# Seven products of half size for pairs 4 to 10 in the first part of the third gated feed-forward stage

## What is computed

```python
f = rmsnorm(h, norm_ffn_g[i])
h = h + (jax.nn.silu(f @ w_gate[i]) * (f @ w_up[i])) @ w_down[i]
```

## Time and profile before

| | us |
|---|---|
| median of 3 runs | 2271.45 |
| lowest, highest | 2271.45, 2273.67 |
| profiled execution | 2273.23 |
| its span | 2272.0 |

### The profile page before, as it was taken

The page is one execution under the profiler, slowest core; times in us unless marked ns, Lnnn a source line. Parts: engine busy times, 40 slices in busy tenths (PEclk is TensorE's granted clock), DMA queues, the critical chain, the costliest instruction groups (busy, mean ns, idle before and its releaser), DMA issues.

```text
span 2272.0 us, 38521 instructions
## 1 busy us (share of the span) xinstructions
PE 2245.7 (99%) x15555; PEld 2017.7 (89%) x15555; DVE 1399.7 (62%) x2549; ACT 1028.0 (45%) x1890; POOL 98.3 (4%) x171
## 2 busy tenths in 40 slices
PE   9999999999999999999999999999999999999998
PEld 7798999999997898999899788978899888888997
DVE  5356576759743465667588566869454465455663
ACT  5256554447533465543376443223244444223652
POOL 3001100000000001000000000100000000000001
PEclk9999999999999999999999999999999999999999
DMA  6545776245434436632365272743222222223651
GB/s 212 157 129 150 187 186 180 98 143 173 135 95 124 116 113 161 196 106 96 115 173 161 81 203 76 189 111 102 93 66 65 66 93 93 93 96 119 185 167 51
DMA packets 90132, 292.78 MB, mean 129 GB/s; under 512 B 12721, under 2 KB 16723, under 8 KB 89187
## 3 DMA queue, kind: packets, MB, share of 16 engines
q1 hardware_dynamic: 79587, 215.69, 29.6%
q0 software_dynamic: 9792, 73.57, 14.0%
q10 hardware_dynamic: 576, 1.05, 0.1%
HBM read 288.14 MB, written 71.34 MB: 158 GB/s over the span
## 4 chain that ended last, share of the span: by engine, by line
PE 88%; DVE 7%; ACT 3%; issue 2%; DMA 0%; POOL 0%; SPq 0%; DVEq 0%; ACTq 0%; POOLq 0%
PE G L1349 61%; PE G L1386 8%; PE G L1459 7%; DVE wL L2334 2%; PE X L1386 1%; PE X L1671 1%; PE X L1626 1%; PE X L1753 1%; PE X L1649 1%; ACT wH L1799 1%; DVE Av L2696 1%; DVE Av L2699 1%; PE X L1737 1%; PE X L1454 1%; PE X L1722 1%
## 5 line engine op out<-in xcount | busy, mean ns | idle before, releaser
L1799 ACT ACTIVATE wH<-raw 128x512 fp32r<-128x512 f32 (+3 forms) x648 | 459.0, 726 | 503.1 <-PE G L1349 429.9
L2334 DVE TENSOR_TENSOR wL<-raw,wH 128x512 fp32r<-128x512 f32 (+3 forms) x648 | 521.3, 815 | 224.8 <-ACT wH L1799 222.0
L1349 PE MATMUL G<-aH,wH 128*128 128x264 f32 (+2 forms) x2112 | 548.2, 321 | 4.4 <-DVE wL L2334 4.1
L1349 PE MATMUL G<-aL,wH 128*128 128x264 f32 (+2 forms) x2112 | 526.5, 311 | 0.0
L1349 PE MATMUL G<-aH,wL 128*128 128x264 f32 (+2 forms) x2112 | 526.2, 311 | 0.0
L1349 PEld LDWEIGHTS G<-aH,wH 128*128 128x128 f32 x2112 | 346.1, 189 | 35.6 <-issue 10.1
L1349 PEld LDWEIGHTS G<-aH,wL 128*128 128x128 f32 x2112 | 344.0, 188 | 22.0
L1349 PEld LDWEIGHTS G<-aL,wH 128*128 128x128 f32 x2112 | 344.6, 188 | 19.1 <-issue 0.2
L2493 DVE TENSOR_TENSOR hT<-G,hT 128x528 f32<-128x528 f32 (+1 forms) x83 | 58.0, 699 | 166.8 <-PE G L1349 166.7
L1386 PE MATMUL G<-seven,wH 128*128 128x264 f32 (+2 forms) x792 | 146.7, 284 | 1.3 <-DVE wL L2334 1.2
L1349 PE MATMUL G<-hidH,wH 128*128 128x264 f32 (+1 forms) x528 | 140.8, 321 | 3.3 <-DVE wL L2334 2.6
(11 more groups left out here) (401 smaller groups left out, 3788.3 us busy)
## 6 DMA issues: line engine op xcount, KB each, us to landing
raw<-weights SPq DMA_DIRECT2D x210, 512.0 KB, 3.7
weight_sums<-weights POOLq DMA_DIRECT2D x72, 704.0 KB, 6.7
raw<-weights SPq DMA_DIRECT2D x48, 704.0 KB, 4.1
raw<-weight_sums SPq DMA_DIRECT2D x132, 256.0 KB, 3.0
raw<-weights SPq DMA_DIRECT2D x99, 256.0 KB, 2.9
weight_sums<-weight_sums POOLq DMA_DIRECT2D x24, 704.0 KB, 4.8
raw<-weights SPq DMA_DIRECT2D x12, 384.0 KB, 6.0
negc<-sums POOLq DMA_DIRECT2D x16, 264.0 KB, 5.7
```

Of the source, the lines that this page charges most:

```text
L1349: done = e.matmul(m.pair(i)[0:M, bank, 0:n], a[:, k, 0:M], b[:, kx, lo - t0:lo - t0 + n], start=(k == 0 and c == 0), stop=(k == nk - 1 and ...
L1799: e.activation(m.high(i)[:, c], m.raw(i)[:, c], ACT.Copy).then_inc(s.w_hi, 1)
L2334: e.tensor_tensor(m.low(i)[:, c], m.raw(i)[:, c], m.high(i)[:, c].bitcast(F32), ALU.subtract).then_inc(s.w_lo, 1)
```

## The change

`SEVEN[2]` goes from 11 to 4: in the first half of the third stage pairs 4 to 10 are made by seven products each. The plain tiles of pairs 0 to 3 stay. The operands are now made in the first half: `early_operands` puts `norm7`, `sum7` and the halves of operands 1, 2, 5 and 6 beside plain tiles `u2` 1 to `g2` 3, and `last_operands` puts the low half of 6 and both halves of 7, 3 and 4 beside the first products, since those lie over `aH` and `aL`, which the plain tiles read. The sources that lay in `low` lie in `scratch`, a part of `hid2H` and `hid2L` that pairs 7 to 10 fill later. The `d2` tiles of the first half have no operand steps beside them any more. The weight sums of seven pairs are added: 32 transfers of 448 KB, and `EVERY` is changed for the last 64.

```diff
-SEVEN = {0: 11, 1: 11, 2: 11}
+SEVEN = {0: 11, 1: 11, 2: 4}
-EVERY = (1.4, 2.5, 3.2)
+EVERY = (1.4, 2.5, 2.3, 2.3)
...
-        for jj in range(0 if half else 11):
+        for jj in range(0 if half else SEVEN[f]):
...
-        for jj, p in by_seven(11 * half):
+        for jj, p in by_seven(0 if half else SEVEN[f]):
...
     def seven():
+        last = deque()
+        if ROLE[state["next"]][1:3] == (2, 0):
+            last.extend(last_operands(2))
...
             for what in splits_at(i):
                 step(*what)
+            if last:
+                for what in last.popleft():
+                    step(*what)
...
+    def early_operands():
+        n, c = [("norm7", 2, j) for j in range(8)], [("sum7", 2, p) for p in (5, 6, 7, 3)]
+        h, w = [("high7", 2, p) for p in (1, 2, 5, 6)], [("low7", 2, p) for p in (1, 2, 5)]
+        return [{2: n[0], 4: n[1], 6: n[2]}, {2: n[3], 4: n[4], 6: n[5]}, {1: n[6], 3: n[7], 6: c[0]}, {2: c[1], 5: c[2]},
+                {1: c[3], 2: h[0], 5: w[0], 6: h[1]}, {1: w[1], 2: h[2], 5: w[2], 6: h[3]}]
+
+    def last_operands(f):
+        return [[(kind + "7", f, p) for kind, p in group] for group in (
+            (("low", 6), ("high", 7)), (("high", 3),), (("low", 7),), (("high", 4),), (("low", 3),), (("low", 4),))]
...
             for half in range(2):
-                if half:
-                    yield from seven()
-                else:
+                if not half:
                     yield from fm(hold=True)
                     yield from fm(hook=("rms", ("ffn2",)))
-                    for _ in range(20):
-                        yield from fm()
-                made = [] if half else operands(2)
+                    for made in early_operands():
+                        yield from fm(before=made)
+                yield from seven()
                 for j in range(8 - half):
-                    yield from fm(before=made[j] if j < len(made) else {})
+                    yield from fm()
...
     def high7(f, p):
         e.wait_ge(s.seven_in, SUMS_IN["norm7", f, 7] if p in (1, 2, 4) else SUMS_IN["sum7", f, p])
+        if f == 2 and p in LYING:
+            e.wait_ge(s.chunk, AT["g2", 0, SEVEN[2] - 1] + 1)
...
         if j == 0:
-            e.wait_ge(s.chunk, AT["g2", 0, 10] + 1 if f == 2 else AT["up", f, 0, 10, 1] + 1)
+            e.wait_ge(s.chunk, AT["u2", 0, 0] + 1 if f == 2 else AT["up", f, 0, 10, 1] + 1)
```

More of the change, by code:

```diff
@@ L46, with by_seven @@
 SUMS = (5, (1, 5)), (6, (5, 3)), (4, (6, 2)), (7, (5, 3))
-EVERY = (1.4, 2.5, 3.2)
+EVERY = (1.4, 2.5, 2.3, 2.3)
 RATE_STATE, RATE_OUT, RATE_FOX, RATE_INDEX, RATE_HEADS = 0.5, 0.75, 0.8, 0.33, 0.62
 LNEXP = "natural_log_exp_and_others"
-def by_seven(pairs):
-    out = [(0, 1), (0, 2), (0, 5)] if pairs else []
-    for jj in range(pairs - 1):
+def by_seven(first):
+    out = [(first, 1), (first, 2), (first, 5)] if first < 11 else []
+    for jj in range(first, 10):
         nx = jj + 1
-        if nx < pairs - 1:
+        if nx < 10:
             out += [(jj, 6), (nx, 1), (jj, 7), (nx, 2), (nx, 5), (jj, 3), (jj, 4)]
@@ L1195, in __init__ @@
         with ExitStack() as c:
+            with ExitStack() as c1:
+                scratch = [sb("scratch0", [128, 11, 512], F32, c1), sb("scratch1", [128, 11, 512], F32, c1)]
             self.hid2H = sb("hid2H", [128, 11, 512], F32R, c)
@@ L1203, in __init__ @@
         self.seven_own, self.source_own, self.source_low = (seven1, seven2), (source1, source2), low
+        self.scratch = [flat(t[:, 7:11, :]) for t in scratch]
     def vc(self, key, j=0, n=1):
@@ L1222, in seven_source @@
         n = STAGE[f][1]
-        if p in LYING:
+        if p in LYING and f == 2:
+            t = self.scratch[LYING[p] % 2][:, 1024 * (LYING[p] // 2):1024 * (LYING[p] // 2) + 1024]
+        elif p in LYING:
             t = self.source_low[:, 1056 * LYING[p]:1056 * LYING[p] + 4 * n]
@@ L1377, in prod7 @@
             e.wait_ge(s.sums_dve, SUMS_DVE[("c22",) + key])
-        if jj == 0:
+        if (half, jj) == ((0, SEVEN[2]) if f == 2 else (1, 0)):
             e.wait_ge(s.seven_lo, NTH["low7", f, p])
@@ L2489, in evac @@
             parts = parts_of(role)
-            if role[0] in ("down", "d2") and role[-2] == 0:
-                e.wait_ge(s.seven_in, SUMS_IN["norm7", 2 if role[0] == "d2" else role[1], role[-1]])
+            if role[0] == "down" and role[-2] == 0:
+                e.wait_ge(s.seven_in, SUMS_IN["norm7", role[1], role[-1]])
             h = split_view(m.hT[:, role[-1], parts[0][1]:L], parts)
```

2 lines of the change are left out of this document (1 added, 1 removed).

## The result

The changed kernel takes 2269.2 us (median; 2267.0 to 2270.9), the kernel before, timed beside it, 2273.0 us (2271.1 to 2275.0), 20 runs of each. The ratio is 0.9982, 95% interval 0.9976 to 0.9989: 0.18% or 4.1 us faster, with an interval from 2.5 to 5.5 us; the two medians lie 3.8 us apart. The forecast was -4.9 us and 2266.5 us; of the 2.7 us between 2266.5 and 2269.2, 1.5 are the median of before, which came out at 2273.0 here and not at 2271.45, and the rest, 1.2, is a sum that was too good. The profiled executions have spans of 2272.0 and 2268.6 us.

What follows compares the result with a forecast made beforehand. TensorE, busy 99% of the span, was taken as the bound. Terms: -7.97 + 3.1 + 0 = -4.9 us, from a median of 2271.45 to 2266.5 us, given 60%; range 2263.3 to 2270.6 us.

Steps and rivals of the forecast that it cites:

- Part 1, the matmuls: Third stage, first half: 14 plain tiles (77.84 us) go, 49 products (69.87 us) come; gain 7.97 us.
- Part 2, operands beside plain tiles: Beside plain tiles 1 to 3: VectorE has 29 of 33.4 us of work, tight but enough; counted as nothing.
- the walk: Step-by-step timing of the engines' queues, beside the plain tiles (least split margin 1.7 us) and at the seam (3.1 us stall).
- Part 3, the seam: New passage from plain tiles to products: TensorE waits before (4,5), (4,6), (4,7); 3.1 us lost, bounds 0 and 6.0.
- The pace of 1.426 us: Time per product, read from the second part's 77 products (109.79 us) and applied to the 49 new ones.
- the second part's products as they are: Third stage, second part: its 77 products were taken as unchanged by the change, at no cost.
- Second seam at no price: Passage from products to `d2`, now occurring twice: TensorE sits idle 0 us there, so no cost.
- Part 4, the transfers: 32 more GpSimd transfers for weight sums, ending near 1640 us ahead of their readers; 0 us, bounds 0 and 0.7.
- No stall at the seam: Rival, 12%: ScalarE and VectorE get through sooner where plain tiles pass to products; 2263.5 us.
- VectorE as the bound beside plain tiles: Rival, 14%: late evacuations or splits beside the plain tiles cost 1 to 4 us more; 2267.5 to 2270.5 us.
- Starved loads: Rival, 8%: between 1495 and 1640 us GpSimd's transfers delay weight loads of some 23 tiles; 2275.6 us, slower.
- The 4.5 us that a measurement can tell: Smallest difference from no change that a measurement of this kernel was said to tell, about 0.2%.

Runs made afterwards that it cites:

- Run A: Not a separate kernel: the stretch of 49 new products up to the first `d2` in the third gated stage; 73.42 us in the changed kernel.
- the idle sums: Kernel before, plus the change's 32 further transfers on GpSimd's queue, their results read by nobody; 2273.9 us (1 run) against 2273.0.
- the kernel with the jump before product 1: Changed kernel with reordered seam steps and third-stage slots skipped singly, plus the first two stages' ring jump moved from product 38 to 1; span 2265.0 us.

## Why the prediction was right, and where it was not

- **Part 1, the matmuls: right.** 7.97 us of gain. With both stalls nearly gone the 49 products take 70.45 us for the 69.87 of the sum. TensorE's weight loads are busy 72.83 of 74 us in that kernel, and whatever they cost is in the pace already, as the prediction argued. The rule of the Trainium skill that spoke against the change (Perfetto Trace Analysis, Identifying the Most-Contended Engine: judge TensorE by the share of peak arithmetic that it reaches and by the busy share of weight loads) does not decide here when its second half is read alone, as the prediction did: in the trace before, a weight load's record lasts 188 ns on average in both stretches, and where matmuls follow at 119 ns such records overlap and fill the row. The other estimate, 8.3 us from the Trainium skill's page TensorE: Matmul & The Clock Gate, Back-to-back issue gap, came close for a poor reason: the page gives that formula for a matmul by itself and says that it misses in a stream of weight loads and matmuls. The rows have 232 and 119 ns where it has 215.8 and 109.2, and the two errors nearly cancel in the difference.
- **Part 2, operands beside plain tiles: right, counted as nothing.** No idle TensorE there: 45.79 busy of 46 us, as before, with VectorE up by 14 us. The tightness was real but the walk had it. The evacuations of the five tiles ahead came 1.9, 0.5, 1.6, 0.1 and 1.2 us late, walked as 1.9, 0.5, 1.6, 0.3 and 1.1; that of `g2` 3, forecast 0.20 us after (4,1), is at 1952.28, just that.
- **Part 3, the seam: right in mechanism, 0.5 us too dear.** Forecast 3.1 us, measured 2.64. The waits came at the three products named and for the three steps named, but not in the three sizes: 1.57, 0.87 and 0.13 us for 1.55, 0.92 and 0.31. The walk's own start of (4,7), 9.91, is 2.78 over the plain pace; the three restarts of 0.3 us were added on top, although the walk's 0.15 us behind each wait held most of them: (4,6), started after a wait, is over in 1.49 us instead of 1.426. The rest is (4,7), walked 9.91 and measured 9.77.
- **"The pace of 1.426 us", in part 1, and "the second part's products as they are": the step that failed.** That pace was read in a run of products that started at slot 3 of the ring and had no jump. The change alters where both runs start; each then loses 0.8 us in its middle, 1.6 us in all, a term that the sum put at nothing. The two stalls of the earlier stages in the trace before (1182.63 and 1184.79 us) were the row that would have priced it. Sum with it: -7.97 + 2.64 + 0.8 + 0.8 + 0.1 for the product behind (4,7), which takes 1.54 us, = -3.6, measured -3.66 in the window. That the forecast was no further off is partly luck: the 0.5 us by which the seam was too dear hid a third of the missing term.
- **Second seam at no price: right.** Run A goes over into `d2` without a gap, and the `d2` tiles take 61.34 us in both kernels.
- **Part 4, the transfers: right, 0 us.** GpSimd issues the last one at 1631.39 us in the changed kernel; with the 6 to 7 us that one takes, the forecast end near 1640 us holds.
- **The rivals.** No stall at the seam: refuted by the rows at 1956.50 and 1958.80, though an order with none exists. VectorE as the bound beside plain tiles: refuted. Starved loads: refuted, by the changed kernel and the idle sums. The range held for a reason that was not foreseen: its upper end, 2270.6 us, was made for waits beside the plain tiles, which did not come, and the 1.6 us of the ring and the 1.5 us by which before itself came out higher used that room.
- **The 4.5 us that a measurement can tell: too coarse.** With 20 runs of each kernel the interval is 1.5 us wide to either side, so a gain of 4.1 us is told from none, although it lies inside the 4.5.

## To carry to other kernels

When a change alters how many items pass through a ring of buffers, write out which slot each later user gets, before and after: users that the change does not touch may change their phase, and a jump that hands out slots after two products instead of five cost 0.8 us a run here, and 1.1 us in the earlier stages. A pace read from a run is the pace of that run's ring positions; look for the same code's worst stretch elsewhere in the trace. The releaser in a bracket is a guess: hold it against the end of the step that it names, as at (4,6) twice. And where a seam is walked and found costly, try another order of the queued steps at once: here three short moves gave back 2.2 of 2.6 us.

## What the runs showed of the chip beyond this

Spans of kernels that are the same up to 480 us differ by up to 2 us, and the table by stretch shows where some of it is. The stretch of 11 to 25 us in the changed kernel, and in the kernel with the jump before product 1:

```profile
11.00:25.00 14.00, 14.00 (x117) 12.88 (x118) 13.04 (x27) 10.88 (x20) 5.98 (x9) 0.88 0.72 271
```

```profile
11.00:25.00 14.00, 14.00 (x110) 12.88 (x111) 13.02 (x27) 10.83 (x20) 6.10 (x9) 0.81 0.73 277
```

The mean granted clock is 0.88 in one and 0.81 in the other, that is, more of the second's 14 us lie at 1.2 GHz and fewer at 2.4; TensorE is busy all the time in both, with seven matmuls fewer in the second. 0.07 x 14 us is 1.0 us. Of the thirteen profiled executions nine stand at 0.88 or 0.89 and four at 0.79 to 0.81; from the first matmul that needs weights, at about 11 us, to the first product near 482 us the nine take 470.1 to 471.0 us, the four 471.9 to 472.1. From 25 us on to the last product near 2190 us the clock is 1.00 in all. Together with the first weights' arrival (10.4 to 11.7 us), that is most of the scatter from run to run. The four are the four kernels in which the first two stages' slots were changed, but the first changed instruction comes after the clock's; what makes the start fall into one or the other was not tried. For reading traces it means: compare windows that begin after the start, not spans, where less than 2 us matter.
